# Third-kind mixers: attention slots spread from the thirteenth chunk on, with the head norm and the products at places of their own

## The reference, cut to what matters

```python
h = rms_norm(x, norm1_g[l])
z = h @ w_in[l]                          # 1024 x 8704
zq, zf, zi, zg, zatt, za, zb = jnp.split(z, split_idx, axis=-1)
o_hg = hgrn2_chunked(q_hg, log_f, k_hg, v_hg)          # a gated linear recurrence, 4 heads
o_hg = rms_norm(o_hg, hg_norm_g[l]...) * sigmoid(zg)   # the head norm
for g, (window, dilation) in enumerate(((128, 1), (512, 4), (2048, 16))):
    ...                                                # rope on q, k; dilated causal window attention, 4 heads of 128
o_att = jnp.sum(softmax(lses) * outs)                  # the three groups merged by their log-denominators
y = sigmoid(za) * (o_hg @ w_branch_a[l]) + sigmoid(zb) * (o_att @ w_branch_b[l])
x = x + y @ w_out[l]
h2 = rms_norm(x, norm2_g[l]); x = x + square(relu(h2 @ w_up[l])) @ w_down[l]
```

## Time and profile before

| | us |
|---|---|
| median of 3 runs | 1978.55 (1977.77 to 1978.79) |
| the profiled execution, its own time | 1981.19 |
| its span, first to last instruction | 1979.4 |

### The profile page before, as it was taken

The page is one execution under the profiler, slowest core; times in us unless marked ns, Lnnn a source line. Parts: engine busy times, 40 slices in busy tenths (PEclk is TensorE's granted clock), DMA queues, the critical chain, the costliest instruction groups (busy, mean ns, idle before and its releaser), DMA issues.

```text
span 1979.4 us, 26113 instructions
## 1 busy us (share of the span) xinstructions
PE 1917.7 (97%) x9981; PEld 1635.1 (83%) x9981; DVE 1273.0 (64%) x1640; ACT 968.6 (49%) x1231; POOL 35.2 (2%) x66
## 2 busy tenths in 40 slices
PE   9999889999999999799999999999999999999998
PEld 7788777888888898588878998778888998788887
DVE  4466677456646556755575896686646787776654
ACT  5454444454445436254545445545434544654543
POOL 1000100000000000000000000000000000000000
PEclk9999999999999989899999999999999999999999
DMA  9556535656665645266555555256555555345552
GB/s 338 180 182 210 177 109 170 192 181 185 208 192 180 190 149 163 73 204 188 178 177 169 163 164 162 104 172 201 179 192 193 182 159 175 108 161 189 174 187 85
DMA packets 173947, 343.55 MB, mean 174 GB/s; under 512 B 11088, under 2 KB 11264, under 8 KB 173712
## 3 DMA queue, kind: packets, MB, share of 16 engines
q1 hardware_dynamic: 169360, 327.26, 51.1%
q0 software_dynamic: 4096, 13.77, 2.1%
q10 hardware_dynamic: 384, 1.05, 0.2%
HBM read 338.36 MB, written 1.05 MB: 171 GB/s over the span
## 4 chain that ended last, share of the span: by engine, by line
PE 87%; DVE 8%; ACT 2%; DMA 1%; issue 1%; POOL 0%; ACTq 0%; SPq 0%; DVEq 0%
PE stream L1968 20%; PE stream L1970 20%; PE stream L1969 20%; PE stream L2135 4%; PE stream L2136 4%; PE stream L2137 4%; PE aux L2015 3%; PE aux L2365 2%; PE stream L2006 1%; DVE wlo L1104 1%; PE stream L2074 1%; PE stream L2076 1%; PE stream L2075 1%; PE stream L1997 1%; PE stream L1998 1%
## 5 line engine op out<-in xcount | busy, mean ns | idle before, releaser
L1104 DVE TENSOR_TENSOR wlo<-raw,whi 128x1024 fp32r<-128x1024 f32 x584 | 707.6, 1223 | 560.3 <-ACT whi L676 556.6
L676 ACT ACTIVATE whi<-raw 128x1024 fp32r<-128x1024 f32 x584 | 612.4, 1057 | 673.3 <-PE stream L1970 537.7
L1968 PE MATMUL stream<-whi,xhi 128*128 128x512 f32 x1168 | 462.0, 396 | 2.4 <-DVE wlo L1104 2.4
L1970 PE MATMUL stream<-whi,xlo 128*128 128x512 f32 x1168 | 456.2, 391 | 0.0
L1969 PE MATMUL stream<-wlo,xhi 128*128 128x512 f32 x1168 | 455.4, 390 | 0.0
L1968 PE MATMUL stream<-whi,hhi 128*128 128x512 f32 x704 | 276.8, 393 | 2.2 <-DVE hlo L1626 1.5
L1970 PE MATMUL stream<-whi,hlo 128*128 128x512 f32 x704 | 274.3, 390 | 0.0
L1969 PE MATMUL stream<-wlo,hhi 128*128 128x512 f32 x704 | 274.0, 389 | 0.0
L1970 PEld LDWEIGHTS stream<-whi,xlo 128*128 128x128 f32 x1168 | 219.7, 188 | 47.0
L1968 PEld LDWEIGHTS stream<-whi,xhi 128*128 128x128 f32 x1168 | 220.0, 188 | 46.3 <-issue 2.4
L1969 PEld LDWEIGHTS stream<-wlo,xhi 128*128 128x128 f32 x1168 | 220.1, 188 | 43.8
(11 more groups left out here) (321 smaller groups left out, 1775.4 us busy)
## 6 DMA issues: line engine op xcount, KB each, us to landing
raw<-ffn_w_gu SPq DMA_DIRECT2D x176, 512.0 KB, 4.4
raw<-w_in SPq DMA_DIRECT2D x136, 512.0 KB, 4.7
raw<-ffn_w_down SPq DMA_DIRECT2D x88, 512.0 KB, 3.6
raw<-w_up SPq DMA_DIRECT2D x64, 512.0 KB, 3.6
raw<-w_down SPq DMA_DIRECT2D x64, 512.0 KB, 3.6
raw<-c_w_in SPq DMA_DIRECT2D x24, 512.0 KB, 4.1
raw<-ab_w_in SPq DMA_DIRECT2D x20, 512.0 KB, 4.8
raw<-w_out SPq DMA_DIRECT2D x16, 512.0 KB, 3.7
```

The source lines that it names most:

```text
L676: act.activation(split_slots(lin, at, j)[0], raw[:, b % RAW], ACT.Copy).then_inc(hi_ready, 1)
L1104: dve.tensor_tensor(lo, raw[:, b % RAW], hi.bitcast(F32), ALU.subtract).then_inc(lo_ready, 1)
L1968: pe.matmul(bank[tt][:], hi, wh, start=kt == 0, stop=False)
L1970: mm = pe.matmul(bank[tt][:], lo, wh, start=False, stop=kt == last)
```

## The change

It replaces the rule of `step_at` by tables of places, counted from block 48 (the first of the thirteenth chunk, c = 12). The same operations are done by the same engines; only their places in the three orders differ, and four buffers lie elsewhere.

| piece | blocks before | blocks after |
|---|---|---|
| slots n = 0 to 8 (8 only turns weights 7) | 52 54 56 58 60 62 64 66 68 | 48 50 52 54 56 59 62 65 68 |
| values m = 0 to 7 | 57 59 61 63 65 67 69 71 | 53 55 57 60 63 66 69 71 |
| head squares | 57 59 | 57 58 |
| head scale | 61 63 | 60 61 |
| head transposes, hi and lo | 65 67 | 64 66 |

```diff
-def step_at(lin, c, j, first):
-    step = first + (c * lin.kb + j) // 2
-    return step if 0 <= step < len(BATCHES_G) + 2 else None
+LOGITS_G = (0, 2, 4, 6, 8, 11, 14, 17, 20)
+VALUES_G = (5, 7, 9, 12, 15, 18, 21, 23)
+SQUARES_G, SCALE_G, TURN_G = (9, 10), (12, 13), (16, 18)
+
+def found(table, at):
+    return table.index(at) if at in table else None
...
-        att = [sb(f"att{i}", [P, 6 * P], at=(24 + 3 * i) * KB) for i in range(2)]
-        att_t = [sb(f"att_t{i}", [P, 6 * P], at=(40 + 3 * i) * KB) for i in range(2)]
+        att = [sb(f"att{i}", [P, 6 * P], at=at * KB) for i, at in enumerate((24, 90))]
+        att_t = [sb(f"att_t{i}", [P, 6 * P], at=at * KB) for i, at in enumerate((40, 28))]
...
-        o_square = sb("o_square", [P, TT, CH], at=90 * KB)
+        o_square = sb("o_square", [P, TT, CH], at=44 * KB)
...
                     def within(c, j):
-                        n = step_at(lin, c, j, first)
-                        if n is None:
-                            return
-                        if j % 2 == 0:
+                        at = first + c * lin.kb + j
+                        n, m, tt = found(LOGITS_G, at), found(VALUES_G, at), found(TURN_G, at)
+                        if n is not None:
...
-                        elif n >= 2:
-                            batch = BATCHES_G[n - 2]
-                            h, = batch.heads
-                            turn_hi(hhi[:, 4 + h:5 + h, batch.tt * P:(batch.tt + 1) * P], 1)
-                        if lin is into and c == 16 and j % 2:
-                            heads_hi(j // 2)
+                        if m is not None:
+                            h, = BATCHES_G[m].heads
+                            turn_hi(hhi[:, 4 + h:5 + h, BATCHES_G[m].tt * P:(BATCHES_G[m].tt + 1) * P], 1)
+                        if tt is not None:
+                            heads_hi(tt)
...
-                layer(into, place, func, after=after, within=beside(into, -26))
-                layer(br_a, lambda c: rows_of(branch_a, c), within=beside(br_a, 8))
+                layer(into, place, func, after=after, within=beside(into, -48))
+                layer(br_a, lambda c: rows_of(branch_a, c), within=beside(br_a, 20))
...
-                        if lin is into and c >= 14 and j % 2:
-                            (head_squares, head_scale, heads_lo)[c - 14](j // 2)
+                        for table, piece in ((SQUARES_G, head_squares), (SCALE_G, head_scale), (TURN_G, heads_lo)):
+                            if at in table:
+                                piece(found(table, at))
...
-                        elif n >= 2:
-                            batch = BATCHES_G[n - 2]
+                        if m is not None:
+                            batch = BATCHES_G[m]
                             h, = batch.heads
-
-                            pe.wait_ge(aux_free, weights_turned[n - 2])
+                            if m == 0:
+
+                                pe.wait_ge(evicted, 2 * (into.c0 + 12) + 2)
+                            pe.wait_ge(aux_free, weights_turned[m])
...
-                        if lin is into and c == 16 and j % 2:
+                        if tt is not None:
                             seen.heads += 1
                             pe.wait_ge(heads_normed, seen.heads)
-                            turn(o_hg[:, j // 2], 0, 4)
+                            turn(o_hg[:, tt], 0, 4)
```

More of the change, by code:

```diff
@@ L1015, in within @@
                                 act.activation(part, part, ACT.Copy, scale=total).then_inc(scaled, 1)
[L1016 removed]
+                            if n:
                                 seen.aux += BATCHES_G[n - 1].banks
[L1018 to L1028 removed]
+                        if m is not None:
[3 more added lines that the diff above has]
+                            heads_hi(tt)
+                    return within
+                layer(into, place, func, after=after, within=beside(into, -48))
+                layer(br_a, lambda c: rows_of(branch_a, c), within=beside(br_a, 20))
                 def turned_hi(half):
@@ L1814, in within @@
                     def within(c, j):
[L1815 to L1818, removed]
+                        at = first + c * lin.kb + j
+                        n, m = found(LOGITS_G, at), found(VALUES_G, at)
+                        if n is not None:
                             if n < len(BATCHES_G):
                                 masked_logits(BATCHES_G[n], n, P ** -0.5, mask)
-                            if 0 < n <= len(BATCHES_G):
+                            if n:
                                 copy_weights(BATCHES_G[n - 1], n - 1)
@@ L1832, in within @@
                             turn_lo(hhi[part], hlo[part], 1)
-                        if lin is into and c >= 14 and j % 2:
-                            (head_squares, head_scale, heads_lo)[c - 14](j // 2)
+                        for table, piece in ((SQUARES_G, head_squares), (SCALE_G, head_scale), (TURN_G, heads_lo)):
+                            if at in table:
+                                piece(found(table, at))
                     return within
-                layer(into, use, beside(into, -26))
+                layer(into, use, beside(into, -48))
                 def gated_a(c):
@@ L1846, in gated_a @@
                                                ALU.mult))
-                layer(br_a, gated_a, beside(br_a, 8))
+                layer(br_a, gated_a, beside(br_a, 20))
                 def branches(c):
@@ L2423, in within @@
                                 mm = pe.matmul(bank[:, 0:P], av[:, g, kt, h * P:(h + 1) * P],
-                                               att_t[n % 2][:, i * P:(i + 1) * P],
+                                               att_t[m % 2][:, i * P:(i + 1) * P],
                                                start=i == 0, stop=i + 1 == len(batch.pieces))
                             mm.then_inc(aux_full, 1)
-                        if lin is into and c == 16 and j % 2:
+                        if tt is not None:
                             seen.heads += 1
                             pe.wait_ge(heads_normed, seen.heads)
-                            turn(o_hg[:, j // 2], 0, 4)
+                            turn(o_hg[:, tt], 0, 4)
                             o_turned.append(seen.aux)
@@ L2435, in mixer_g @@
                 layer(into, xhi, xlo, after=after,
-                      major=lambda c: "columns" if c in (1, 2) or 4 <= c < 10 else "rows", within=beside(into, -26))
-                layer(br_a, hhi, hlo, ready=lambda j, tt: (aux_free, o_turned[tt]), within=beside(br_a, 8))
+                      major=lambda c: "columns" if c in (1, 2) or 4 <= c < 10 else "rows", within=beside(into, -48))
+                layer(br_a, hhi, hlo, ready=lambda j, tt: (aux_free, o_turned[tt]), within=beside(br_a, 20))
                 o_at = seen.aux
```

## The result

The changed kernel takes 1980.63 us (median of 20 runs, 1977.82 to 1982.93), the kernel before 1977.72 (20 runs, 1974.67 to 1980.67). The ratio is 1.0014, with a 95% interval of 1.0008 to 1.0019: about 2.9 us slower, which is within 0.2% and clear of zero. The forecast was 1982.5, that is 4.0 us above the 1978.55 it started from. It missed 1980.63 by 1.9 us: 0.8 because the median before came out lower over 20 runs than over the first 3, and 1.1 because the forecast difference was too large.

What follows compares the result with a forecast made beforehand. PE's stream of matmuls plus its waits was taken to bound the kernel. Waits (+0.7) and clock (+1.3) in each of two mixers, added to 1978.55, gave 1982.5 us; own range 1980.5 to 1984.5, 8-in-10 range 1976 to 1986.5.

Steps and rivals of the forecast that it cites:

- The most that could be won: Blocks 62 to 66: PE's old waits, with DVE late, lose some 5.3 us a mixer, 10.6 in all.
- Slots 0 to 3 at 0 us: Chunk 12: these slots, four blocks earlier, fit in DVE's idle time; cost 0, bounds 0 and 1 us a mixer.
- The addresses: Buffers that lie elsewhere after the change: cost 0.
- The new wait at block 60 and its sum: DVE idles some 3 us behind ACT, then does head scale; PE waits 4.1 us in block 62, 3.5 at values 4.
- The wait at the head's bank: Second bank of weights 6, after head transposes at 64 and 66: PE waits 1.8 us, listed as 1.4 to 1.8.
- The sum without the clock: Per mixer: 5.3 us of old waits go, 4.1 + 1.8 = 5.9 come: +0.7; both mixers +1.4.
- The clock: PE's clock falls to 1.2 GHz at the new wait, costing 1.1 to 2.8 us a mixer; 1.3 taken.
- The sum: Both mixers, waits and clock: 1978.55 + 2 x (0.7 + 1.3) = 1982.5 us; chance 0.42.
- the first rival: Waits come as worked out, but the clock falls in one mixer or none: say 1980.5 us; chance 0.28.
- The second: Room ends the waits if ACT makes values 3's high part before the eviction: 1968.0 to 1971.5 us; chance 0.13.
- The third: Early slots hold PE, transposes of weights 0 and 1 coming before their scaling: 1984.5 us; chance 0.10.
- The fourth: Clock stays low longer, the second wait making it fall again: 3.4 us more in one or both mixers, 1986 to 1989; chance 0.07.

Runs made afterwards that it cites:

- respaced: Changed kernel with slot 5 at block 58, slot 6 at 61, head scale behind slot 6's logits, later slots, values and head transposes moved; ratio to the kernel before 0.9948.
- early_only: Changed kernel with only the four tile-0 slots early (48 50 52 54); slots 4 to 8 and head norm as in the kernel before; ratio to that 0.9992.
- fill_short: Changed kernel with 7 unread matmuls (14 passes, 3.0 us) put in front of PE's wait for values 4; ratio to the kernel before 1.0003.
- val3_58: Changed kernel with one place changed, values 3 at block 58 in place of 60; ratio to the kernel before 1.0017.

## Why the prediction was right, point by point

- **The most that could be won**, 5.3 us a mixer, was right: `respaced`, where PE never waits, wins 5.0 to 5.3.
- **Slots 0 to 3 at 0 us**: right. No wait in chunks 12 and 13, in the changed kernel or in `early_only`. That they win 0.9 us a mixer by themselves, as `early_only` shows, was not in the prediction. The addresses (three buffers lie elsewhere: `att1`, `att_t1` and `o_square`) were put at 0 as well. No run tests them alone, but `respaced` has them too, and PE doesn't wait there.
- **The new wait at block 60 and its sum**: right. DVE idle "some 3 us" is 2.86, PE's wait is listed as 3.32 for 3.2 to 3.3, and block 62 lost 8.71 - 4.70 = 4.0 us for 4.1. Both parts that I put on the chain, ACT's loads and the head scale, are shown to be on it by leaving each out.
- **The wait at the head's bank**, 1.8 us lost: with the clock up, in `fill_short`, slot 7 and its block take 1264.61 - 1258.36 = 6.25 us where 4.70 were due, so 1.55 are lost. It was sized 0.25 too long. The profile was to list it as 1.4 to 1.8; it lists 1.33 with the clock up, and 0.88 in the changed kernel itself, where the slow clock takes up part. That sign was missed.
- **The sum without the clock**, +0.7 a mixer: +0.33 by `fill_short`. This is the first term that was mis-sized: 0.25 is the head's bank, 0.1 is block 62.
- **The clock**: it fell in all four mixers that I profiled of the changed kernel, as it had at the six long waits of before. The Trainium skill, on its page TensorE: Matmul & The Clock Gate (HAM oscillation), says that gaps in a stream of matmuls put the clock back; the trace agrees, with PEclk 0.58 and 0.71 at these waits of 3.32 us. I took 1.3 us from bounds of 1.1 to 2.8. The falls of 3.4 us, three of the four, cost 1.1 to 1.2; that of 6.8 cost 2.3. So the bounds were right, and 1.3 is near the short kind. My reason for the low end, that much of a longer fall would lie in the wait itself, held in small part only: some 1 us of the 6.8 did.
- **The sum**: 2 x (0.33 + 1.15) = 3.0 us where both falls are short, and the measured difference is 2.9 (interval 1.6 to 3.8). The forecast of 4.0 was too high by the 0.37 a mixer of the waits and 0.15 a mixer of the clock. With the mean of the four falls, 1.45, the sum is 3.6, which the interval allows too.
- **The number alone would mislead.** 1980.63 lies nearer to the first rival's 1980.5 (the clock falls in one mixer or in none) than to the forecast's 1982.5. That is chance: the median before was 0.8 us lower over more runs, and the waits were smaller than worked out. The traces, not the time, tell the two apart.
- **The rivals**: the first is not what the two profiled executions show; with no fall at all it would have been `fill_short`, 1.0003. The second named a wrong condition, as `val3_58` shows; its other side was there to be had, but by placing slots 5 to 8, the values and the head norm otherwise. The third is excluded. The fourth was not seen: the clock fell once in each mixer, not again at the second wait.

What stays open: why a fall lasts 3.4 us in one execution and 6.8 in another. And `respaced` was not taken apart further, so how much each of the places that it moves brings is not known.

## What to carry to other kernels

More room between slots helps only if the room isn't filled with what all wait for. Lay out the in-order queue of each engine over the stretch, with durations from the trace, and look for a place where one engine's long serial piece (here eviction, two table loads and a root) is followed by another engine's work that had been waiting for it, all ahead of what frees PE's banks. Put first what releases the bound engine, and leave what nobody waits for soon (here the head scale) for the shade of the other engine's work.

When a long wait replaces several short ones of the same sum, add the clock: in this kernel the fall of the clock that came with 3.3 us in one piece cost 1.1 to 2.3 us, and beside pieces of 1.5 us and less in the same stretch there was no fall.

## What the runs showed of the hardware that I had not expected

A float32 matmul of 256 columns with plain float32 operands took two records of 0.216 us each (26 records for 13 matmuls), so filling work has to be counted by the rows of the profile. And a wait of 3.3 to 3.9 us amid dense matmuls came with a clock of 1.2 GHz in six mixers of six (the changed kernel in two executions, `val3_58` in one), while waits of up to 1.67 us in `early_only` left it at 2.4.

The length of a wait is not all that decides. Elsewhere in the kernel before, the clock also fell behind waits of 1.84 us (it ends at 325.87) and 1.70 us (at 1042.64), and not behind one of 1.83 us (at 289.50). What sets these apart no run here tests. The stretches around their ends:

```profile
291.00:295.00 4.00, 3.00 (x15) 2.31 (x14) 3.79 (x9) 3.97 (x11) 0.00 (x0) 1.00 0.00 0
325.00:329.00 4.00, 3.13 (x14) 2.64 (x15) 2.82 (x5) 1.13 (x2) 0.00 (x0) 0.78 0.02 4
1042.00:1046.00 4.00, 3.11 (x13) 2.49 (x14) 2.24 (x5) 1.08 (x2) 0.53 (x1) 0.76 0.01 4
```
